# Down projections of the feed-forward stages: four pairs of row tiles through seven block products instead of eight

## The reference

```python
D_MODEL = 1024; SEQ = 512; D_FF = 2816; DEPTH = 2

def swiglu(h, w_gate, w_up, w_down):
    return (jax.nn.silu(h @ w_gate) * (h @ w_up)) @ w_down

for l in range(DEPTH):
    h = rms_norm(x, gn[0])
    x = x + 0.5 * rms_norm(swiglu(h, w_ffn1_gate[l], w_ffn1_up[l], w_ffn1_down[l]), gn[1])
    ...                                  # mixer
    h = rms_norm(x, gn[4])
    x = x + 0.5 * rms_norm(swiglu(h, w_ffn2_gate[l], w_ffn2_up[l], w_ffn2_down[l]), gn[5])
```

## Time and profile before

| | |
|---|---|
| Time, median of 3 runs | 2660.74 us (2660.72 to 2660.79) |
| Profiled execution, its own time | 2660.73 us |
| Its span, first to last instruction | 2658.9 us |
| PE busy | 2646.9 us (100%) |
| DVE busy | 1821.9 us (69%) |
| ACT busy | 1345.8 us (51%) |
| Mean granted TensorE clock | 0.999 |

### The profile page before, as it was taken

One profiled execution on the slowest core, in us unless ns is written; L12 is line 12 of the kernel. 1 busy time (PEld: TensorE's weight loads), 2 busy tenths in 40 slices (PEclk: granted clock), 3 DMA queues, 4 the chain that ended last, 5 costly groups with the idle time before them and its releaser, 6 DMA issues.

```text
span 2658.9 us, 45273 instructions
## 1 busy us (share of the span) xinstructions
PE 2646.9 (100%) x17836; PEld 1738.7 (65%) x17836; DVE 1821.9 (69%) x2792; ACT 1345.8 (51%) x2300; POOL 136.4 (5%) x119
## 2 busy tenths in 40 slices
PE   9999999999999999999999999999999999999999
PEld 6886476654688746886476654688746566465664
DVE  7995385666799628995375656799625886458854
ACT  5664265552566425664265543566424664346452
POOL 1000012100100001000012100100000002000020
PEclk9999999999999999999999999999999999999999
DMA  5443321213344333443322213444433132322312
GB/s 170 112 122 110 123 76 60 92 64 103 96 111 117 120 103 96 111 112 121 116 71 72 92 64 102 126 113 110 126 103 127 64 96 80 111 70 78 111 64 87
DMA packets 313358, 266.23 MB, mean 100 GB/s; under 512 B 8796, under 2 KB 276316, under 8 KB 312576
## 3 DMA queue, kind: packets, MB, share of 16 engines
q1 hardware_dynamic: 310192, 254.31, 31.3%
q10 hardware_dynamic: 2416, 7.84, 1.1%
q0 software_dynamic: 608, 2.11, 0.3%
HBM read 257.40 MB, written 4.21 MB: 98 GB/s over the span
## 4 chain that ended last, share of the span: by engine, by line
PE 97%; DVE 2%; DVEq 0%; DMA 0%; ACT 0%; issue 0%; SPq 0%; ACTq 0%
PE pu L490 15%; PE pu L491 15%; PE pu L492 15%; PE pm L490 6%; PE pm L492 6%; PE pm L491 6%; PE pu L615 6%; PE pu L614 6%; PE pu L613 6%; PE pm L613 2%; PE pm L614 2%; PE pm L615 2%; PE pm L939 2%; PE pm L685 2%; PE pm L912 1%; PE pm L953 1%
## 5 line engine op out<-in xcount | busy, mean ns | idle before, releaser
L1132 DVE SCALAR_TENSOR_TENSOR w_lo<-stage,w_hi 128x2048 f16<-128x2048 f32 (+1 forms) x152 | 342.8, 2255 | 366.9 <-ACT w_hi L1917 363.1
L1917 ACT ACTIVATE w_hi<-stage 128x2048 f16<-128x2048 f32 (+1 forms) x143 | 265.9, 1859 | 526.5 <-PE pm L492 377.9
L490 PE MATMUL pu<-h_hi,w_hi 128*128 128x512 f16 x912 | 346.3, 380 | 0.0
L492 PE MATMUL pu<-h_hi,w_lo 128*128 128x512 f16 x912 | 345.7, 379 | 0.0
L491 PE MATMUL pu<-h_lo,w_hi 128*128 128x512 f16 x912 | 345.7, 379 | 0.0
L492 PE MATMUL pu<-w_hi,arena 128*128 128x512 f16 x512 | 194.1, 379 | 0.0
L490 PE MATMUL pm<-w_hi,arena 128*128 128x512 f16 x512 | 194.1, 379 | 0.0
L491 PE MATMUL pm<-w_lo,arena 128*128 128x512 f16 x512 | 194.1, 379 | 0.0
L490 PE MATMUL pu<-w_hi,arena 128*128 128x512 f16 x512 | 194.1, 379 | 0.0
L491 PE MATMUL pu<-w_lo,arena 128*128 128x512 f16 x512 | 194.1, 379 | 0.0
L492 PE MATMUL pm<-w_hi,arena 128*128 128x512 f16 x512 | 194.0, 379 | 0.0
(11 more groups left out here) (348 smaller groups left out, 6215.5 us busy)
## 6 DMA issues: line engine op xcount, KB each, us to landing
stage<-in_w_in_dram SPq DMA_DIRECT2D x144, 512.0 KB, 4.6
stage<-in_w_ffn_gate_dram SPq DMA_DIRECT2D x88, 512.0 KB, 4.0
stage<-in_w_ffn_up_dram SPq DMA_DIRECT2D x88, 512.0 KB, 5.2
stage<-in_w_ffn_down_dram SPq DMA_DIRECT2D x80, 512.0 KB, 4.0
stage<-in_w_out_dram SPq DMA_DIRECT2D x40, 512.0 KB, 4.3
stage<-in_w_ffn_down_dram SPq DMA_DIRECT2D x16, 256.0 KB, 4.1
stage<-in_w_branch_hgrn_dram SPq DMA_DIRECT2D x8, 512.0 KB, 3.5
stage<-in_w_branch_attn_dram SPq DMA_DIRECT2D x8, 512.0 KB, 4.5
```

Source lines behind the costliest of these rows:

```text
L490: nc.tensor.matmul(ps, w1, r_hi, start=first, stop=False)
L492: return nc.tensor.matmul(ps, w2, r_hi, start=False, stop=last)
L1132: V.scalar_tensor_tensor(out=w_lo[:, s, 0:n], in0=stage[:, s, 0:n], scalar=WSCALE, in1=w_hi[:, s, 0:n], op0=ALU.mult, op1=ALU.subtract).th ...
L1917: A.activation(w_hi[:, s, 0:n], stage[:, s, 0:n], ACT.Copy, scale=WSCALE).then_inc(hi_split, 1)
```

## The change

Row tiles 14 to 21 become four pairs. In each half, plain slots cover tiles 0 to 13 (4, 4, 3 and 3 tiles) and two slots cover two pairs each. A pair is a 2x2 block product: two row tiles by two column quarters (256 columns) of the weights, and two row tiles by two token halves (256 tokens) of the activations. It is done with seven products of blocks instead of eight (`PRODUCTS`), of 256 columns each. The order of slots is in `DOWN_ORDER`.

- Four 256-wide sums of activations a pair (`form_whole`, `form_sums`, `form_low` on VectorE, `form_high` on ScalarE) go to `af_hi`, `af_lo`, in the memory of `h_hi`, `h_lo`. They are made around slots 0 to 3.
- Each pair slot needs the sums of weight blocks that the fast units also need (`weight_sums`, `low_direct`, `low_sums`, `direct`, `high_sums`), and loads in four transfers (`pair_slot`) instead of two.
- The seven products of both pair slots of a half add up in seven banks. Half 0's plain part is copied out of its banks by ScalarE (`keep_half`); two products are copied by ScalarE (`grab_products`) and the rest joined on VectorE (`combine`). TensorE waits for these steps (`y0_kept`, `comb`, `y_park`) before it takes a bank again.
- Half 0's two parts are added in `add_half`. Half 1's pairs run before its plain slots, so the last banks are added to `y1s` per token block in the new `turn_down`, one more VectorE add a block ahead of the sum of squares.

```diff
-DOWN = (3, 3, 4, 4, 4, 4)
-DOWN_FIRST = (0, 3, 6, 10, 14, 18)
+DOWN = ((0, 4), (4, 4), (8, 3), (11, 3))
+DOWN_PAIRS = ((0, 1), (2, 3))
+PAIRS, PAIR_FIRST = 4, 14
+QUARTER = 256
+DOWN_ORDER = ((0, DOWN[0]), (0, DOWN[1]), (0, DOWN[2]), (0, DOWN[3]), (0, DOWN_PAIRS[0]), (0, DOWN_PAIRS[1]),
+              (1, DOWN_PAIRS[0]), (1, DOWN_PAIRS[1]), (1, DOWN[2]), (1, DOWN[3]), (1, DOWN[0]), (1, DOWN[1]))
+PRODUCTS = ((True, 2, 0), (True, 3, 1), (False, 0, 4), (False, 1, 5), (True, 0, 3), (False, 2, 2), (True, 1, 6))
...
@@ TensorE @@
+                b0, b1, b2, b3 = banks
+                o0, o1, o2, o3 = old
+                pe.wait_ge(evac, t.now("evac") + 1)
+                for i in range(4):
+                    plain_slot(i, banks)
+                pe.wait_ge(evac, t.now("evac") + 2)
+                pe.wait_ge(a_ready, t.next("a_ready", KF))
+                paired_half((o0, o1, o2, o3, b0, b1, b2), 0)
+                paired_half((b3, o0, o1, o2, o3, b0, b1), 1)
+                pe.wait_ge(y_park, t.now("y_park") + 2)
+                for i in range(8, 10):
+                    plain_slot(i, old)
+                tail(old, xn, (slot_ks(DOWN[0]), slot_ks(DOWN[1])), acc, False)
...
+                    pe.wait_ge(split, t.next("split"))
+                    if half_ == 0:
+                        pe.wait_ge(af_ready, t.next("af_ready", len(pairs)))
+                    for n, (own, at, quarter) in enumerate(PRODUCTS):
+                        if n == 2:
+                            pe.wait_ge(split_s, t.next("split_s"))
+                        if i == 0 and half_ == 0 and n >= 4:
+                            pe.wait_ge(y0_kept, t.now("y0_kept") + n - 3)
+                        if i == 0 and half_ == 1 and n != 2:
+                            if n == 0:
+                                pe.wait_ge(y0_kept, t.next("y0_kept", 4))
+                            else:
+                                pe.wait_ge(comb, t.now("comb") + max(1, n - 1))
...
@@ VectorE @@
                 for s in range(2):
...
-                    lo(s, DOWN[s] * HD)
+                    lo(s, DOWN[s][1] * HD)
...
+                form_whole(0)
+                form_sums(0)
+                form_whole(1)
+                form_low(0)
+                form_sums(1)
+                form_whole(2)
+                form_low(1)
                 for i in range(10):
                     t.next("unit_done")
-                    lo(i % 2, DOWN[(i + 2) % 6] * HD)
+                    s, what = i % 2, DOWN_ORDER[i + 2][1]
+                    if what in DOWN_PAIRS:
+                        weight_sums(s, PAIR_LAND)
+                        low_direct(s)
+                        low_sums(s)
+                    else:
+                        lo(s, what[1] * HD)
+                    if i == 0:
+                        form_sums(2)
+                        form_whole(3)
+                        form_low(2)
+                    if i == 1:
+                        form_sums(3)
+                        form_low(3)
+                    if i == 4:
+                        combine(y1s, (o0, o1, o2, o3, b0, b1, b2), (comb,) * 6)
                     if i == 5:
-                        park(banks, 4.0)
+                        add_half()
+                    if i == 6:
+                        combine(y1s, (b3, o0, o1, o2, o3, b0, b1), (comb,) * 2 + (y_park,) * 4)
+                    if i == 7:
+                        park_sums(4.0)
                 t.next("unit_done")
-                turn(old, xn, post, gain)
+                turn_down(old, xn, gain)
+            def turn_down(banks, src, gain):
+                lo_first(0)
+                add(0)
+                gain_half(0)
+                add(1)
+                update(0)
+                gain_half(1)
+                update(1)
+                pre(src, 0)
+                pre(src, 1)
+                add(2)
+                lo_first(1)
+                split_h(banks, 0, 0, gain)
+                split_h(banks, 0, 1, gain)
+                add(3)
+                gain_half(2)
+                update(2)
+                gain_half(3)
+                update(3)
+                split_h(banks, 0, 2, gain)
+                split_h(banks, 0, 3, gain)
+                pre(src, 2)
+                pre(src, 3)
...
@@ ScalarE @@
                 for s in range(2):
-                    hi(s, DOWN[s] * HD)
+                    hi(s, DOWN[s][1] * HD)
                     silu(s)
...
+                form_high(0)
+                form_high(1)
                 for i in range(10):
-                    hi(i % 2, DOWN[(i + 2) % 6] * HD)
-                    if i == 5:
-                        squares(banks)
-                turn(old, gain, 4.0)
+                    s, what = i % 2, DOWN_ORDER[i + 2][1]
+                    if i == 3:
+                        keep_half(banks)
+                    if what in DOWN_PAIRS:
+                        s_.wait_ge(land[s], t.next(f"land{s}", PAIR_LAND))
+                        s_.wait_ge(unit_done, t.next("unit_done"))
+                        direct(s, 512, 2048).then_inc(hi_split, 1)
+                        high_sums(s, 0, 4)
+                    else:
+                        hi(s, what[1] * HD)
+                    if i < 2:
+                        form_high(2 + i)
+                    if i == 4:
+                        grab_products((o0, o1, o2, o3, b0, b1, b2))
+                    if i == 6:
+                        grab_products((b3, o0, o1, o2, o3, b0, b1))
+                    if i == 7:
+                        sum_squares()
+                turn(old, gain, 4.0, True)
```

More of the change, by code:

```diff
@@ L422, in down_slot, with pair_slot @@
                 half(s, 2 * HD, src[:, first + 2:first + n, cols], n - 2, HD)
+            def pair_slot(s, src, pairs, first_col):
+                n, first = len(pairs), PAIR_FIRST + 2 * pairs[0]
+                for e, col in enumerate((first_col + QUARTER, first_col)):
+                    for r in range(2):
+                        half(s, (2 * e + r) * n * QUARTER, src[:, first:first + 2 * n, col:col + QUARTER].rearrange("p (i r) n -> p r i n", r=2)[:, r], n, QUARTER)
             def ffn(l, which):
@@ L486, in _, with product @@
             t = Tally(split=2)
[L488 to L492, removed]
+            def product(ps, w1, w2, r_hi, r_lo, first, last, shared=False):
+                nc.tensor.matmul(ps, w1, r_hi, start=first, stop=False, skip_group_check=shared)
+                nc.tensor.matmul(ps, w1, r_lo, start=False, stop=False, skip_group_check=shared)
+                return nc.tensor.matmul(ps, w2, r_hi, start=False, stop=last, skip_group_check=shared)
             def weights(s, at):
@@ L671, in ffn @@
                         for b in range(NB):
-                            last = token_part((banks if i < 6 else old)[b], b, i % 2, [(at, k)], acc, k == 0, k == KF - 1)
+                            last = token_part(where[b], b, i % 2, [(at, k)], acc, i in (0, 8) and at == 0, i == 3 and at == what[1] - 1)
                     last.then_inc(unit_done, 1)
-                tail(old, xn, (slot_ks(4), slot_ks(5)), acc, False)
-                t.next("a_ready", KF)
+                b0, b1, b2, b3 = banks
@@ new lines, in add_half, with park_sums @@
+            def add_half():
+                v.drain()
+                v.wait_ge(y0_kept, t.next("y0_kept", NB))
+                for b in range(NB):
+                    V.tensor_tensor(y0g[:, b], y1s[:, b], y0g[:, b], ALU.add).then_inc(y_add, 1)
+                v.drain()
+            def park_sums(q):
+                v.wait_ge(gp_land, t.next("gp_land", 16))
+                for b in range(NB):
+                    v.wait_ge(y0_sq, t.next("y0_sq"))
+                    V.scalar_tensor_tensor(out=y0g[:, b], in0=y0g[:, b], scalar=DS, in1=gp[:, 0:HD], op0=ALU.mult, op1=ALU.mult)
+                v.drain()
+                V.tensor_scalar(st[:, 0], st[:, 0], q / D, q * EPS, ALU.mult, ALU.add).then_inc(bias_ready, 1)
```

163 lines of the change are left out of this document (143 added, 20 removed).

## The result

The changed kernel takes 2645.13 us, the median of 4 runs (2644.84 to 2645.41), against 2660.73 (2660.72 to 2660.79) in the same session: a ratio of 0.9941, 95% interval 0.9929 to 0.9953. The prediction was 2644.5, so it is 0.6 us off, in a change of 15.6. The profiled execution took 2645.27 us with a span of 2643.4 at a mean clock of 0.999; its span is 15.5 us shorter than that of before.

The account below looks back on a forecast made before the run. TensorE was taken to bound the down stages. Four stages of -4.77 (matmuls) + 0.40 (first slot) + 0.30 (turn) gave -16.3 us, from 2660.73 to 2644.5 us, range 2641 to 2652.

Parts of the forecast that it names:

- What bounds the kernel; matmuls removed: Down stages: TensorE bounds; 336 narrow matmuls (36.7 us) replace 192 wide (41.4 us), gaining 4.77 us a stage.
- A longer first slot: Slot 0's longer high part on ScalarE delays the last fast unit's first grab; TensorE loses 0.40 us a stage.
- Forms of activations: Slots 0 to 3: VectorE's new sums stay hidden behind TensorE, costing nothing, smallest margin 1.1 us.
- Pair slots: 9.17 us each; weight sums and combine on VectorE cost TensorE nothing, margins of 1.0 us and more.
- Rival 2: TensorE waits at slot 8 for combine's fourth step, 1.0 us a stage: 2648.5 us; chance 0.13, including both with rival 1.
- The turn: Behind each down stage: VectorE's extra adds delay the chain to TensorE's transposes; 0.30 us lost a stage.
- Rival 1: The turn passes its full 1.5 us of lateness a stage to TensorE: 2649.4 us; chance 0.12.
- Rival 4: Narrow products don't run at half price, 0.206 us a matmul with loads on top: 2775 us; chance 0.01.
- Rival 3: VectorE's form adds run slow, making VectorE the bound; TensorE stands 17.8 us a stage: 2715 us; chance 0.03.
- The sum: Four stages of -4.77 + 0.40 + 0.30 give -16.3 us, from 2660.73 to 2644.5 us.

Follow-up runs that it names:

- eight: Changed kernel with the seventh product of each pair slot done twice, so eight products a pair; 2665.62 us (one run).
- silu_first: Changed kernel with ScalarE doing the silu and first grab of the last fast unit ahead of slot 0's high part; 2643.17 us, ratio 0.9934.
- forms_late: Changed kernel with four more VectorE adds of 1024 and drains (5.2 us) ahead of the forms of activations; 2664.72 us (one run).
- delay3: Changed kernel with three unused VectorE adds of 1024 and drains (counted at 3.84 us) ahead of the second combine; 2652.59 us (one run).
- no_add: Changed kernel without the turn's adds of half 1's pair sums, so its output is incomplete; 2643.59 us (one run).
- late_turn: Changed kernel with the turn's fourth group of transposes moved behind the next stage's first matmuls; 2645.75 us, ratio 0.9943.
- pool_silu: silu_first with half 1's gain multiplies in the turn (four of 512 a stage) moved from VectorE to GpSimd; 2648.32 us, ratio 0.9953.
- both: Changed kernel with the edits of silu_first and late_turn together; 2644.30 us, ratio 0.9938.
- delay1: Changed kernel with one unused VectorE add of 1024 and a drain (counted at 1.28 us) ahead of the second combine; 2645.87 us (one run).

## Why the prediction was right

**What bounds the kernel; matmuls removed.** Right to 0.02 us: 36.68 us for 336 narrow matmuls against the predicted 36.7. Taking the price from the fast units, which have the same shape and as many weight loads, was the choice that decided the sum. The distances that the prediction takes from the Trainium skill (TensorE: Matmul & The Clock Gate, Back-to-back issue gap), 131 ns at 512 columns and midway 98 ns at 256, were not found here: it is 215.8 ns by the earlier trace rows, and 109.2 in the pair slots, as in the earlier trace rows. eight shows that the narrow form alone would have lost.

**A longer first slot.** Right: 0.39 to 0.40 us a stage against 0.40. silu_first removes it by the order on ScalarE alone, so its cause is shown, not only argued. It was a loss of that order, not of the change.

**Forms of activations.** The layout was right to 0.1 us at slot 2 and at slot 3 of the second stage. VectorE's timeline of the changed kernel in the second stage, whose slot 0 begins at 898.51:

```profile
914.61 1.76 DVE L1212 SCALAR_TENSOR_TENSOR w_lo<-stage,w_hi 128x1536 f16<-128x1536 f32 x1
...
921.01 1.76 DVE L1212 SCALAR_TENSOR_TENSOR w_lo<-stage,w_hi 128x1536 f16<-128x1536 f32 x1 [0.40 <-ACT w_hi L2140]
...
949.89 0.68 DVE L1415 TENSOR_TENSOR arena<-pu,arena 128x512 f32<-128x512 f32 x1
...
961.96 2.50 DVE L1436 TENSOR_TENSOR arena<-arena 128x512 f32<-128x512 f32 x4
964.55 1.76 DVE L1212 SCALAR_TENSOR_TENSOR w_lo<-stage,w_hi 128x1536 f16<-128x1536 f32 x1
```

The low part of slot 2 ends 17.9 us after slot 0 begins (predicted 17.9), that of slot 3 24.3 (24.2). In the first stage it is 20.1 instead of 19.6, wanted at 20.7, and the difference is one of VectorE's pauses of 0.45 us, which stands among the form steps there (ahead of 241.87). That leaves the smallest margin of the change, 0.6 by the timeline; forms_late, where the pause at that step is 0.17, has 0.8.

**Pair slots.** Counting from slot 5 at 943.94, the first `comb` comes at 6.6 (predicted 7.3), `add_half` ends at 20.5 (21.2), slot 8's low part at 22.4 (22.9). All of it is 0.5 to 0.7 us earlier than predicted, and the slack of VectorE at slot 8 is 2.3 us (2.0 in the first stage), not 1.7. Rival 2's wait isn't there; delay3 shows that it is the right wait, and that it would take 2 us more of VectorE's work to bring it about.

**The turn.** The place and the mechanism were right, the size a little low and the split wrong. The slack at the first transposes is 0.57 us, as predicted (0.5). The wait of the bank is 0.31 in place of 0.2, and the tenth of a microsecond given to `h_lo` and the last `xn` rows is not there in three turns; in one it is 0.35, through a pause of VectorE, which the prediction didn't reckon with. In all 4 x 0.31 + 0.35 = 1.6 us against 1.2. That the 0.30 a stage came so near the 0.31 is luck in part: it was added up from 0.2 and 0.1. Rival 1's 1.5 us a stage doesn't appear, because the slack was there. no_add shows that the adds cause the 0.31 us, late_turn that a later use of the banks by TensorE doesn't mend it.

**Rivals 3 and 4.** Rival 4 is excluded by the pair slots. Rival 3 didn't happen, and GpSimd is idle in the down stage. That GpSimd is the other party was only taken for granted in the prediction; the trace of before bears it out. The add of the earlier trace rows took 2.99 us there not once but three times in 16 (at 709.53, 1033.73 and 1708.96), each time beginning 1.1 us into a GpSimd add of 3.03 us, and the 1.76 us lost are again the time to that add's end less 0.15. pool_silu brings the same about on purpose, 1.0 us a step. The rival's price was understated, though: it counted TensorE's standing alone, and in forms_late each of four gaps of 2.4 to 4.4 us cost 1.6 to 2.3 us more through the clock.

**The sum.** Predicted -16.3. Found -15.5 between the spans and -15.6 between the medians: 0.4 for the turn, and 0.45 for a late landing at the start, which the change does not cause and which differs from execution to execution.

## What to carry to other kernels

Where a stage is bound by TensorE, price its matmuls by the distance of starts of the same shape elsewhere in the trace. Then write the other engines' queues out step by step against the slots: it held here to 0.7 us. When a step ahead of a short, urgent one grows, put the urgent one first; and where a chain of adds on VectorE is the cause of a wait, changing the consumer's order or handing a part to GpSimd didn't help, only less work in that chain did.

## What the runs showed of the hardware

- When TensorE had stood for 2.4 to 4.4 us, its granted clock went to half (1.2 GHz), and 3.3 to 4.7 us of its work ran at half, 1.6 to 2.3 us lost each time (four gaps of forms_late). With 1.8 to 2.1 us it did not (four gaps of delay3), as the window behind the longest of them shows:

```profile
301.80:305.00 3.20, 3.17 (x15) 1.49 (x16) 3.12 (x4) 2.19 (x8) 0.00 (x0) 1.00 0.00 0
```

- In the second stage of forms_late the clock was still full for the first matmuls after the gap and fell about a microsecond later, so a slow stretch has to be looked for behind the gap that causes it.
- In these traces a VectorE step with both inputs in SBUF that began beside a GpSimd multiply or add took longer by nearly the rest of GpSimd's instruction: 1.0 us beside a multiply of 1.27 us (pool_silu, twelve times), 1.76 us when it begins 1.1 us into an add of 3.03 us (before, three times).
- VectorE at times pauses for 0.4 to 0.5 us with nothing to wait for, eleven times in the changed kernel (241.87, 339.37, 924.50 and 1324.30 lie in its down stages and turns). The place goes with the program: in the changed kernel and in silu_first, late_turn, both and eight, where VectorE's instructions are the same, the pauses stand before the same eleven instructions, and in the versions that add or drop VectorE instructions they stand elsewhere behind the first such edit (in delay1 one lies in the second turn, at 1016.87, and TensorE stands 0.31 us there). Other executions of one and the same program were not traced. Where slack is under half a microsecond, an edit elsewhere in VectorE's program can so bring a wait about or take it away. In the changed kernel an 8 KB transfer of the profile's queue 14 (kind "instruction") begins 0.7 to 3.6 us behind the end of each of the eleven; whether the two belong together was not tested, and the cause stays open.
